# Value and output weights taken by halves of rows, inputs in quarters on two queues, and one more expert weight requested early

## The chip, the cores and the metric

The kernel runs on one core of a Trainium2 chip. The metric is the device time of one execution in microseconds; the median of three is 1227.86. TensorE (PE) does the matrix products, VectorE (DVE) and ScalarE (ACT) the elementwise work, GpSimd (POOL) a little of it, and SyncE (SP) issues nearly all loads.

## The reference, cut to what matters

All arrays are float32: 256 tokens, width 1024. The part around the change is the first mixer, and behind it a mixture of 32 experts and a second block.

```python
proj = h @ w_in[l] + b_in[l]          # 1024 x 5632
hg_q, hg_f, hg_i, hg_g, mb_q, mb_k, mb_v, gate_a, gate_b = jnp.split(proj, split_at, axis=-1)
y_a = hgrn2_mixer(hg_q, hg_f, hg_i, hg_g, ...) @ w_proj_a[l]
y_b = moba_mixer(mb_q, mb_k, mb_v, rel_bias) @ w_proj_b[l]
mixed = (jax.nn.sigmoid(gate_a) * y_a + jax.nn.sigmoid(gate_b) * y_b) @ w_out[l]
x = layer_norm(DN_ALPHA * h + mixed, ln1_g[l], ln1_b[l])
ffn = hier_moe(x, w_group[l], ...)    # 32 experts, two for each token
x = layer_norm(DN_ALPHA * x + ffn, ln2_g[l], ln2_b[l])
return second_block(x, ...)
```

## The kernel before, in words

All weights come as numbered units of 1 MB: unit i, 128 partitions x 2048 numbers. Units 0 to 25 are w_in and the two projections, 26 to 29 are w_out, and from E0 = 30 on come the experts' weights, 192 of them. For most units of the first stage a float32 product is made of three products in a rounded format (fp32r): ACT rounds the unit (`round_hi`, tile hi), DVE takes the rest (`rest_lo`, tile lo), and PE does hi*hi, hi*rest and rest*hi, 48 matmuls with 256 moving columns for one unit. Units 0 and 1 go through PE directly, out of tile xraw (x transposed) and raw. There are three buffers for hi and three for lo, six (raw0 to raw5) for the units themselves.

Most units are stationary on PE, with x moving. Those whose result has the tokens on partitions are moving instead: values i (4, 5), values mv (10, 11) and w_out (26 to 29). Each of these is a slice of 256 columns by all 1024 rows. `moving` does one such tile, `project_n` calls it for the values, `out_tile(j, i, k0, k1)` does slice j of w_out for half i of the tokens and rows from 128*k0 to 128*k1. Between rows 0 to 511 and 512 to 1023 of slice 0, PE does 18 small matmuls with the router's weights (WRG, called S12 below, L663 and L664).

DVE works in the order of the code: it copies S12 out of PSUM (L2046), then makes lo of units 27, 28 and 29 (L1850), then adds the residual for tokens 0 to 127 (L2118) once slices 0 to 3 of that half are done, norms, and goes on to the router.

SP issues loads strictly in order. A load into a buffer waits until its last user has left it: a raw buffer of the first stage is left when lo of its unit is made. The experts' units have a ring of 21 buffers: nine "spare" ones in areas of the first stage (semaphores early0 to early8), the six raw ones, and six "half" ones in the areas of hi and lo. Units E0 to E0+2 go to spare buffers once the attention is done; E0+3 to E0+6 go to raw0 to raw3, each behind lo of units 24 to 27; then E0+7 and E0+8 to spare ones. From E0+21 on a load waits for PE to have used the unit of 21 places before.

At the start SP issues half of x, half of unit 0, the other half, then unit 1; ACT issues the other half of x. PE keeps itself busy with four products of zeros (L533) until these are in.

Of the kernel before, what the change touches and what calls it, by code (L numbers as in the profile page):

```python
# [137 lines left out]
def weight_units(t):  # L138
# [17 lines left out]
    for j in range(4):  # L156
        units.append(("w_out", j, tcols(t["w_out"], (0, D), 256 * j, 256), 256, 8))
# [40 lines left out]
def memory(nc, t):  # L198
# [122 lines left out]
    K.RO = [sb(f"RO{n}", 1024, A0 + 40 * KB + 4 * KB * n) for n in range(4)]  # L321
    K.RZ = sb("RZ", 1024, A0 + 56 * KB)
# [126 lines left out]
def moving(pe, K, i, o, ks, xh, xl, start=True, stop=True):  # L449

    h, l, n = K.hi[i % HN], K.lo[i % HN], K.units[i][3]
    for c, k in enumerate(ks):
        pe.matmul(o, xh(k), K.view(h, n * c, [[1, 256]]), start=start and c == 0, stop=False)  # L453
        pe.matmul(o, xl(k), K.view(h, n * c, [[1, 256]]), start=False, stop=False)  # L454
        r = pe.matmul(o, xh(k), K.view(l, n * c, [[1, 256]]), start=False, stop=stop and c == len(ks) - 1)  # L455
    return r


def pe_mixers(pe, K, S):
# [72 lines left out]
    for n in range(4):  # L532
        pe.matmul(bank(7, 0, [1, 256]), view(K.QE, 0, [[1, 128]]), view(K.QE, 0, [[1, 256]]), start=True, stop=True)  # L533
# [100 lines left out]
    def out_tile(j, i, k0, k1):  # L634
        n = 26 + j
        if i == 0 and k0 == 0:
            lo_done(pe, K, S, n)
        b = 4 + 2 * i + j // 2
        h, l = K.hi[n % HN], K.lo[n % HN]
        if b == 7:  # L640
            pe.wait_ge(S.dve_step, STEP["s12"])
        for k in range(k0, k1):
            if j == 0 and k % 2 == 0:
                pe.wait_ge(S.mx_lo, k // 2 + 1)
            x, y = (view(m, 256 * k + 128 * i, [[1, 128]]) for m in (K.MXH, K.MXL))
            o = bank(b, 256 * (j % 2), [1, 256])
            pe.matmul(o, x, view(h, 256 * k, [[1, 256]]), start=k == 0, stop=False)
            pe.matmul(o, y, view(h, 256 * k, [[1, 256]]), start=False, stop=False)
            r = pe.matmul(o, x, view(l, 256 * k, [[1, 256]]), start=False, stop=k == 7)
        if k1 == 8 and i == 1:  # L650
# [1209 lines left out]
def dve_mixers(dve, K, S, own):  # L1860
# [3 lines left out]
    for n in range(2):  # L1864
        dve.wait_ge(S.early1 if n else S.early0, 16)
# [27 lines left out]
    def project(u):  # L1893
        dve_ahead(dve, K, S, u, K.E0)
        nm, j = K.units[u][:2]
        if nm in ("i", "mv"):
# [3 lines left out]
            dve.tensor_tensor(view(x, 256 * j, [[512, 2], [1, 256]]), bank(u % 3, 0, [256, 2], [1, 256]),  # L1900
                              view(K.BIA, (512 if nm == "mv" else 0) + 256 * j, [[0, 2], [1, 256]]), ALU.add).then_inc(S.pj_dve, 1)
# [209 lines left out]
def dve_router(dve, K, S, own):  # L2111
# [842 lines left out]
```

## Time and profile before

| | us |
|---|---|
| median of three executions | 1227.86 |
| lowest, highest | 1227.84, 1228.46 |
| the profiled execution | 1226.06 |
| its span on the core | 1224.8 |
| PE busy in it | 1093.8 |
| DVE busy in it | 581.4 |
| ACT busy in it | 476.8 |

Times in the trace count from the span's start. Three stages can be told apart: up to about 232 us the first mixer and the router, up to about 672 us the experts, and then the second block. PE's records overlap (one matmul of 256 columns lasts 0.28 us, but the next starts 0.12 us later), so pace is read from starts, not from durations.

### The profile page before, as it was taken

How to read it: one execution, taken by the hardware profiler on the slowest of the kernel's cores; microseconds unless marked ns; L12 is line 12 of the kernel's file. 1: busy time of each engine (PE TensorE's matmuls, PEld its weight loads, DVE VectorE, ACT ScalarE, POOL GpSimd, SP SyncE). 2: the span in 40 equal slices, each digit the busy share in tenths (PEclk: the TensorE clock that was granted, in tenths of full speed). 3: DMA queues.
4: the chain of work that ended last, by engine and by line, in shares of the span. 5: the costliest groups of instructions: out<-in, count | busy, mean ns of one | idle time of the engine just before them, and what ended most of it. 6: DMA issues, size and time to landing. Idle time of an engine off the chain costs nothing.

```text
span 1224.8 us, 22361 instructions
## 1 busy us (share of the span) xinstructions
PE 1093.8 (89%) x9746; PEld 907.8 (74%) x9746; DVE 581.4 (47%) x856; ACT 476.8 (39%) x650; POOL 87.7 (7%) x92
## 2 busy tenths in 40 slices
PE   8999999997767666666678999999999999999998
PEld 7999999764333333332324799999999999999998
DVE  4765676633222121212112766564554547666643
ACT  5644763221111111111123744433357775544432
POOL 1440000000000000000000400000110005000011
PEclk9999999999797878887977999999999999999999
DMA  9943567999999999999999766544534236565520
GB/s 336 324 144 111 189 226 298 421 419 421 420 421 420 420 422 420 420 421 419 412 422 409 234 207 200 179 155 169 193 103 156 87 105 201 177 207 175 177 97 35
DMA packets 144688, 329.82 MB, mean 269 GB/s; under 512 B 5507, under 2 KB 115388, under 8 KB 119886
## 3 DMA queue, kind: packets, MB, share of 16 engines
q1 hardware_dynamic: 142528, 321.99, 69.6%
q10 hardware_dynamic: 1470, 4.29, 1.0%
q0 software_dynamic: 592, 2.10, 0.5%
q8 instruction: 78, 1.28, 0.4%
q14 instruction: 20, 0.16, 0.0%
HBM read 327.30 MB, written 1.06 MB: 268 GB/s over the span
## 4 chain that ended last, share of the span: by engine, by line
PE 64%; DMA 31%; DVE 2%; ACT 1%; issue 1%; SPq 0%; DVEq 0%; ACTq 0%
PE PS L443 15%; PE PS L444 15%; PE PS L445 15%; DMA half<-in_w_down_dram 11%; DMA half<-in_w_gate_up_dram 7%; DMA raw<-in_w_down_dram 5%; DMA spare<-in_w_down_dram 4%; DMA raw<-in_w_gate_up_dram 4%; PE PS L785 3%; PE PS L453 1%; PE PS L454 1%; PE PS L455 1%; PE PS L771 1%; PE PS L526 1%; DVE lo L1850 1%; PE PS L1265 1%
## 5 line engine op out<-in xcount | busy, mean ns | idle before, releaser
L1850 DVE TENSOR_TENSOR lo<-raw,hi 128x2048 fp32r<-128x2048 f32 (+1 forms) x112 | 253.1, 2266 | 141.6 <-ACT hi L1357 112.6
L1357 ACT CAST hi<-raw 128x2048 fp32r<-128x2048 f32 (+1 forms) x110 | 203.7, 1857 | 102.4 <-PE PS L445 90.1
L443 PE MATMUL PS<-AH,hi 128*128 128x256 f32 (+1 forms) x816 | 234.8, 288 | 1.3 <-DVE AL L2339 1.0
L445 PE MATMUL PS<-AH,lo 128*128 128x256 f32 (+1 forms) x816 | 232.6, 285 | 0.0
L444 PE MATMUL PS<-AL,hi 128*128 128x256 f32 (+1 forms) x816 | 232.3, 285 | 0.0
L443 PEld LDWEIGHTS PS<-AH,hi 128*128 128x128 f32 x816 | 153.9, 189 | 2.7 <-issue 1.0
L445 PEld LDWEIGHTS PS<-AH,lo 128*128 128x128 f32 x816 | 154.0, 189 | 0.0
L444 PEld LDWEIGHTS PS<-AL,hi 128*128 128x128 f32 x816 | 153.5, 188 | 0.4
L2267 DVE TENSOR_TENSOR Y<-PS,Y 32x256 fp32r<-32x256 f32 x128 | 53.9, 421 | 131.8 <-ACT Y L1562 128.8
L2258 DVE TENSOR_TENSOR T<-T,PS 64x256 f32<-64x256 f32 x32 | 13.5, 423 | 192.8 <-ACT T L1554 192.7
L444 PE MATMUL PS<-FL,hi 128*128 128x272 f32 (+1 forms) x352 | 100.3, 285 | 0.0
L443 PE MATMUL PS<-FH,hi 128*128 128x272 f32 (+1 forms) x352 | 100.0, 284 | 0.0
L445 PE MATMUL PS<-FH,lo 128*128 128x272 f32 (+1 forms) x352 | 99.8, 284 | 0.0
L1562 ACT CAST Y<-PS 32x256 fp32r<-32x256 f32 x128 | 46.4, 363 | 132.0 <-PE PS L785 128.0
L1554 ACT ACTIVATE T<-PS 64x256 f32<-64x256 f32 x32 | 12.1, 377 | 205.6 <-PE PS L785 205.6
L785 PE MATMUL PS<-raw,XS 128*32 128x256 f32 x720 | 54.5, 437 | 22.7 <-DMA raw<-in_w_gate_up_dram 22.5
L785 PE MATMUL PS<-half,XS 128*32 128x256 f32 x640 | 53.8, 479 | 23.3 <-DMA half<-in_w_gate_up_dram 20.4
L443 PE MATMUL PS<-XH,hi 128*128 128x256 f32 x256 | 74.5, 291 | 0.0
L785 PE MATMUL PS<-spare,XS 128*32 128x256 f32 x688 | 50.0, 420 | 26.4 <-DMA spare<-in_w_gate_up_dram 26.4
L445 PE MATMUL PS<-XH,lo 128*128 128x256 f32 x256 | 72.4, 283 | 0.0
L444 PE MATMUL PS<-XL,hi 128*128 128x256 f32 x256 | 72.4, 283 | 0.0
L445 PEld LDWEIGHTS PS<-FH,lo 128*128 128x128 f32 x352 | 66.4, 189 | 0.0
(419 smaller groups left out, 1950.1 us busy)
## 6 DMA issues: line engine op xcount, KB each, us to landing
raw<-in_w_gate_up_dram SPq DMA_DIRECT2D x45, 1024.0 KB, 27.0
spare<-in_w_gate_up_dram SPq DMA_DIRECT2D x43, 1024.0 KB, 26.7
half<-in_w_gate_up_dram SPq DMA_DIRECT2D x40, 1024.0 KB, 27.0
half<-in_w_down_dram SPq DMA_DIRECT2D x23, 1024.0 KB, 26.4
raw<-in_ffn_w_gate_dram SPq DMA_DIRECT2D x22, 1024.0 KB, 5.6
raw<-in_ffn_w_up_dram SPq DMA_DIRECT2D x22, 1024.0 KB, 5.6
raw<-in_w_in_dram SPq DMA_DIRECT2D x21, 1024.0 KB, 10.8
raw<-in_w_down_dram SPq DMA_DIRECT2D x21, 1024.0 KB, 27.6
```

Of the source, the lines that this page charges most:

```text
L443: pe.matmul(o, w(h, c), xh(k), start=start and c == c0, stop=False)
L444: pe.matmul(o, w(h, c), xl(k), start=False, stop=False)
L445: r = pe.matmul(o, w(l, c), xh(k), start=False, stop=stop and c == c0 + len(ks) - 1)
L453: pe.matmul(o, xh(k), K.view(h, n * c, [[1, 256]]), start=start and c == 0, stop=False)
L454: pe.matmul(o, xl(k), K.view(h, n * c, [[1, 256]]), start=False, stop=False)
L455: r = pe.matmul(o, xh(k), K.view(l, n * c, [[1, 256]]), start=False, stop=stop and c == len(ks) - 1)
L785: r = pe.matmul(bank(b, 0, [1, 256], p0=32 * c, rows=32), x, view(w[0], w[1] + 256 * c, [[1, 256]]), start=first, stop=last)
L1357: act.copy(K.view(K.hi[i % HN], 0, [[1, n]]), K.view(K.rbuf[i], 0, [[1, n]])).then_inc(S.hi, 1)
L1562: act.copy(view(K.Y, 256 * c, [[1, 256]], 64 * (e % 2), KEEP), bank(down_bank(e), 0, [1, 256], p0=32 * c, rows=KEEP)).then_inc(S.y_hi, 1)
L1850: r = e.tensor_tensor(K.view(K.lo[i % HN], 0, [[1, n]]), K.view(K.rbuf[i], 0, [[1, n]]), K.view(K.hi[i % HN], 0, [[1, n]]).bitcast(F32), A ...
L2258: dve.tensor_tensor(K.T1[:, :], K.T1[:, :], bank(GB + e % 2, 0, [1, 256], p0=64, rows=64), ALU.mult).then_inc(S.hm, 1)
L2267: dve.tensor_tensor(l, bank(down_bank(e), 0, [1, 256], p0=32 * c, rows=KEEP), h.bitcast(F32), ALU.subtract).then_inc(S.y_lo, 1)
```

## The change

The units of values i and mv and of w_out become 512 rows by 512 columns instead of 1024 rows by 256 columns, so PE runs 24 matmuls of 512 moving columns for each instead of 48 of 256. A pair of values' units now fills two PSUM banks, one for each half of tokens, and DVE takes both out after the second unit. For w_out, units 26 and 27 are rows 0 to 511 (columns 0 to 511, and 512 to 1023), 28 and 29 are rows 512 to 1023. S12 stands behind both halves of tokens of unit 26. `w_in` is laid out in memory as 22 tiles that are contiguous for each partition (8 KB). The two halves of x and of unit 0 become four quarters each, x all on ACT's queue, unit 0 on SP's, and the zero products are three instead of four. E0+3 goes to a spare buffer with E0 to E0+2, and the raw buffers and all others shift by one place; areas of later tiles move so that this spare buffer is free. In the router, DVE adds the residual of tokens 128 to 255, columns 0 to 511, after the statistics of the first half of tokens.

```diff
+        w, c = (512, 4) if nm in ("i", "mv") else (256, 8)
         for j in range(2):
-            units.append((nm, j, tcols(win, (0, D), c0 + 256 * j, 256), 256, 8))
+            units.append((nm, j, win[c0 // 256 + j].rearrange("p (c n) -> p c n", c=c), w, c))
...
-        units.append(("w_out", j, tcols(t["w_out"], (0, D), 256 * j, 256), 256, 8))
+        units.append(("w_out", j, tcols(t["w_out"], (512 * (j // 2), 512 * (j // 2) + 512), 512 * (j % 2), 512), 512, 4))
...
-    ring = early[:3] + own[:4] + early[3:5] + own[4:] + early[5:]
+    ring = early[:4] + own[:4] + early[4:5] + own[4:] + early[5:]
...
-    for c, k in enumerate(ks):
-        pe.matmul(o, xh(k), K.view(h, n * c, [[1, 256]]), start=start and c == 0, stop=False)
+    for c, k in enumerate(ks, c0):
+        pe.matmul(o, xh(k), K.view(h, n * c, [[1, n]]), start=start and c == c0, stop=False)
...
-    for n in range(4):
+    for n in range(3):
         pe.matmul(bank(7, 0, [1, 256]), view(K.QE, 0, [[1, 128]]), view(K.QE, 0, [[1, 256]]), start=True, stop=True)
...
-    out_tile(0, 0, 0, 4)
-    out_tile(0, 1, 0, 4)
+    out_tile(0, 0)
+    out_tile(0, 1)
...
-    out_tile(0, 0, 4, 8)
-    out_tile(0, 1, 4, 8)
-    out_tile(1, 0, 0, 8)
-    out_tile(1, 1, 0, 8)
-    out_tile(2, 0, 0, 8)
-    out_tile(3, 0, 0, 8)
-    out_tile(2, 1, 0, 8)
+    out_tile(1, 0)
+    out_tile(1, 1)
+    out_tile(2, 0)
+    out_tile(3, 0)
+    out_tile(2, 1)
 
     pe.wait_ge(S.mx_mul, 8)
-    for n, (i, k0, k1) in enumerate(TURNS[:2]):
-        turn_rows(pe, K, S, n, i, k0, k1)
-    out_tile(3, 1, 0, 8)
+    turn_rows(pe, K, S, 0, *TURNS[0])
+    out_tile(3, 1, 0, 2)
+    turn_rows(pe, K, S, 1, *TURNS[1])
+    out_tile(3, 1, 2, 4)
...
-    act.dma_start(half(K.xraw, 1), t["xT"][:, 1024:2048]).then_inc(S.early1, 16)
+    for q, sx in enumerate((S.early0, S.early1, S.early2, S.early3)):
+        act.dma_start(view(K.xraw, 512 * q, [[1, 512]]), t["xT"][:, 512 * q:512 * q + 512]).then_inc(sx, 16)
...
-    dve.wait_ge(S.unit, 28)
-    residual(1, 0, 512)
     dve.wait_ge(S.x1_r, 1)
     for c in range(2):
         r = dve.bn_stats(st(0, 6 * c, 6), rows(0, 512 * c, 512))
     factor(0, own(r))
+    dve.wait_ge(S.unit, 29)
+    residual(1, 0, 512)
...
-    sp.dma_start(view(K.xraw, 0, [[1, 1024]]), t["xT"][:, :1024]).then_inc(S.early0, 16)
+    for q, sw in enumerate((S.early4, S.early5, S.early6, S.early7)):
+        sp.dma_start(view(K.raw[0], 512 * q, [[w, 2], [1, w]]), w0[:, 2 * q:2 * q + 2, :]).then_inc(sw, 16)
...
-    for i in range(7):
+    for i in range(8):
         sp_load(sp, K, S, K.E0 + i)
```

PE, before, from the first matmul of w_out to the first of unit 27. In the names, hi_57 and lo_60 hold unit 26, hi_55 and lo_58 unit 27.

```order
L647 MATMUL PS<-hi_57,MXH 128x256 [waits mx_lo,lo]
...
L647 MATMUL PS<-hi_57,MXH 128x256 [waits mx_lo]
...
L663 MATMUL PS<-WRG,cm 128x80 [waits rows,cm,mo_lo,pool_step]
L663 MATMUL PS<-WRG,cm 128x80 x7
L664 MATMUL PS<-rowp,cm 128x40
L647 MATMUL PS<-hi_57,MXH 128x256 [waits mx_lo]
...
L647 MATMUL PS<-hi_55,MXH 128x256 [waits lo]
```

PE, after, the same place (L455 is the first line of `moving`).

```order
L455 MATMUL PS<-hi_57,MXH 128x512 [waits mx_lo,lo]
...
L664 MATMUL PS<-WRG,cm 128x80 [waits rows,cm,mo_lo,pool_step]
L664 MATMUL PS<-WRG,cm 128x80 x7
L665 MATMUL PS<-rowp,cm 128x40
L455 MATMUL PS<-hi_55,MXH 128x512 [waits lo]
L456 MATMUL PS<-hi_55,MXL 128x512
...
L455 MATMUL PS<-hi_55,MXH 128x512 [waits dve_step]
```

Before, 24 matmuls of 256 columns stand ahead of S12 and 24 between it and unit 27. After, 24 matmuls of 512 columns stand ahead of it and none between it and unit 27.

DVE, after, around S12 (tile S_106; lo_58, lo_59 and lo_60 are units 27, 28 and 29).

```order
L2048 TENSOR_TENSOR MXL<-SGA,MXH 128x512 [waits mx_hi] x2
L2051 TENSOR_SCALAR S_106<-PS 128x40 [waits pe_step]
L2052 COPY S_106<-PS 128x40
L1852 TENSOR_TENSOR lo_58<-raw_52,hi_55 128x2048 [waits unit,hi,raw3]
L1852 TENSOR_TENSOR lo_59<-raw_53,hi_56 128x2048 [waits unit,hi,raw4]
```

This order on DVE is that of before: lo of unit 27 still follows the copies of S12.

SP, after, the first loads of the experts (raw_49 to raw_52 are raw0 to raw3).

```order
L2669 DMA spare_188<-in_w_gate_up_dram 128x2048
L2669 DMA spare_189<-in_w_gate_up_dram 128x2048
L2669 DMA raw_49<-in_w_gate_up_dram 128x2048 [waits lo]
L2669 DMA raw_50<-in_w_gate_up_dram 128x2048 [waits lo]
L2669 DMA raw_51<-in_w_gate_up_dram 128x2048 [waits lo]
L2669 DMA raw_52<-in_w_gate_up_dram 128x2048 [waits lo]
L2669 DMA spare_190<-in_w_down_dram 128x2048 [waits mx_lo]
```

Before, spare_189 stood behind raw_52, the load that waits for lo of unit 27; now it stands ahead of raw_49.

## Rows read from the trace of the kernel before

**Rows 1.** The page, parts 1 and 2: busy share; GB/s in 40 slices.

```profile
PE 1093.8 (89%) x9746; PEld 907.8 (74%) x9746; DVE 581.4 (47%) x856; ACT 476.8 (39%) x650; POOL 87.7 (7%) x92
...
GB/s 336 324 144 111 189 226 298 421 419 421 420 421 420 420 422 420 420 421 419 412 422 409 234 207 200 179 155 169 193 103 156 87 105 201 177 207 175 177 97 35
```

**Rows 2.** The chain that ended last: start, us, what.

```profile
14.57 6.91 PE PS L478 x32
...
264.04 24.24 DMA spare<-in_w_down_dram
```

**Rows 3.** Windows, all engines: us, PE, PEld, DVE, ACT, POOL busy, PEclk, DMA, GB/s.

```profile
192.00:196.00 4.00, 4.00 (x37) 4.00 (x35) 3.25 (x5) 1.29 (x4) 1.85 (x2) 1.00 0.18 70
196.00:200.00 4.00, 4.00 (x34) 3.87 (x33) 3.08 (x5) 1.88 (x2) 0.00 (x0) 1.00 0.01 2
...
204.00:208.00 4.00, 4.00 (x36) 4.00 (x35) 1.06 (x1) 0.00 (x0) 0.00 (x0) 1.00 1.03 430
```

**Rows 4.** Timeline of the start: start us, us, engine, line, operation, count.

```profile
2.64 3.78 PE L533 MATMUL PS<-QE 128*128 128x256 f32 x8 [2.64 <-POOL KE L2566]
...
7.43 7.14 PE L471 MATMUL PS<-xraw,raw 128*128 128x256 f32 x32 [1.01 <-DMA raw<-in_w_in_dram]
```

**Rows 5.** Windows at the start, same columns.

```profile
3.00:4.00 1.00, 1.00 (x3) 0.81 (x3) 0.00 (x0) 0.00 (x0) 0.00 (x0) 1.00 1.03 406
```

**Rows 6.** Timeline of PE: values (256 columns), second block (272), experts (512).

```profile
36.39 0.28 PE L454 MATMUL PS<-hi,XL 128*128 128x256 f32 x1
36.51 0.28 PE L455 MATMUL PS<-lo,XH 128*128 128x256 f32 x1
...
729.75 0.29 PE L443 MATMUL PS<-AH,hi 128*128 128x272 f32 x1
...
730.88 0.29 PE L443 MATMUL PS<-AH,hi 128*128 128x272 f32 x1
...
265.11 0.85 PE L833 MATMUL PS<-Y,SEL 128*128 128x512 f32 x3
265.34 0.63 PE L833 MATMUL PS<-Y,SEL 128*128 128x512 f32 x2
```

**Rows 7.** Timeline of PE around S12.

```profile
195.36 0.90 PE L663 MATMUL PS<-WRG,cm 128*128 128x80 f32 x7
...
197.54 0.39 PE L647 MATMUL PS<-hi,MXH 128*128 128x256 f32 x1
```

**Rows 8.** Timeline of DVE, from the last rest of the mix to the last residual.

```profile
195.34 1.46 DVE L2043 TENSOR_TENSOR MXL<-SGA,MXH 128x512 fp32r<-128x512 f32 x2
197.64 0.20 DVE L2046 TENSOR_SCALAR S<-PS 128x40 f32<-128x40 f32 x1 [0.84 <-PE PS L664]
197.76 0.19 DVE L2047 COPY S<-PS 128x40 f32<-128x40 f32 x1
197.87 4.49 DVE L1850 TENSOR_TENSOR lo<-raw,hi 128x2048 fp32r<-128x2048 f32 x2
...
212.24 1.82 DVE L2118 SCALAR_TENSOR_TENSOR X<-xtok,PS 128x1024 f32<-128x1024 f32 x2 [7.17 <-PE PS L649]
...
219.30 0.69 DVE L2118 SCALAR_TENSOR_TENSOR X<-xtok,PS 128x512 f32<-128x512 f32 x1 [0.33 <-PE PS L649]
```

**Rows 9.** Timeline of SP: issues of the experts' loads E0, E0+6, E0+20, E0+21.

```profile
173.20 0.34 SPq L2664 DMA_DIRECT2D spare<-in_w_gate_up_dram  x1
...
200.18 0.33 SPq L2664 DMA_DIRECT2D raw<-in_w_gate_up_dram  x1
...
228.25 0.33 SPq L2664 DMA_DIRECT2D spare<-in_w_down_dram  x1
...
236.07 0.33 SPq L2664 DMA_DIRECT2D spare<-in_w_down_dram  x1
```

**Rows 10.** DMA issues of 228 to 229 us: KB, us from issue to landing.

```profile
spare<-in_w_down_dram SPq DMA_DIRECT2D x1, 1024.0 KB, 12.8
```

**Rows 11.** Windows in the router, columns as in rows 3.

```profile
226.00:227.00 1.00, 0.30 (x2) 0.00 (x0) 0.87 (x8) 0.00 (x0) 0.00 (x0) 1.00 1.05 434
...
228.00:232.00 4.00, 3.90 (x16) 2.85 (x15) 3.54 (x19) 0.20 (x1) 0.00 (x0) 0.58 1.01 422
```

More of the change, by code:

```diff
@@ L320, in memory @@
     K.OVX = sb("OVX", OVR, A0 + 8 * KB)
[L321 to L322 removed]
+    K.RO = [sb(f"RO{n}", 1024, A0 + 56 * KB + 4 * KB * n) for n in range(4)]
+    K.RZ = sb("RZ", 1024, A0 + 72 * KB)
     K.SCR = sb("SCR", 1024, A0 + 72 * KB)
@@ L380, in memory @@
     own = [(K.raw[i], f"raw{i}") for i in range(RN)] + [(halves[i], f"half{i}") for i in range(6)]
-    ring = early[:3] + own[:4] + early[3:5] + own[4:] + early[5:]
+    ring = early[:4] + own[:4] + early[4:5] + own[4:] + early[5:]
     K.rbuf, K.filled, K.slot_before = {}, {}, {}
-    count = {f"early{i}": 1 for i in range(4)}
+    count = {f"early{i}": 1 for i in range(8)}
     last = {"raw0": 0}
@@ L464, in first @@
     def first():
+        quarters = ((S.early0, S.early4), (S.early1, S.early5), (S.early2, S.early6), (S.early3, S.early7))
         for k in range(8):
-            if k % 4 == 0:
-                for n in (S.early1, S.early3) if k else (S.early0, S.early2):
+            if k % 2 == 0:
+                for n in quarters[k // 2]:
                     pe.wait_ge(n, 16)
@@ L632, in pe_mixers, with out_tile @@
             r.then_inc(S.unit, 1)
-    def out_tile(j, i, k0, k1):
+    def out_tile(j, i, c0=0, c1=4):
         n = 26 + j
-        if i == 0 and k0 == 0:
+        if i == 0:
             lo_done(pe, K, S, n)
-        b = 4 + 2 * i + j // 2
-        h, l = K.hi[n % HN], K.lo[n % HN]
-        if b == 7:
+        b = 4 + 2 * i + j % 2
+        if j == 1 and i:
             pe.wait_ge(S.dve_step, STEP["s12"])
[L642 to L650, printed above, removed]
+        if i == 0 and j % 2 == 0:
+            pe.wait_ge(S.mx_lo, j + 2)
+        r = moving(pe, K, n, bank(b, 0, [1, 512]), range(4 * (j // 2) + c0, 4 * (j // 2) + c1), lambda k: view(K.MXH, 256 * k + 128 * i, [[1, 128]]),
+                   lambda k: view(K.MXL, 256 * k + 128 * i, [[1, 128]]), start=j < 2, stop=j >= 2 and c1 == 4, c0=c0)
+        if c1 == 4 and i == 1:
             r.then_inc(S.unit, 1)
-        elif j == 3:
+        elif j == 3 and i == 0:
             r.then_inc(S.pe_step, 1)
-    out_tile(0, 0, 0, 4)
-    out_tile(0, 1, 0, 4)
+    out_tile(0, 0)
+    out_tile(0, 1)
     pe.wait_ge(S.pool_step, STEP["wrg"])
@@ L1864, in dve_mixers @@
     for n in range(2):
-        dve.wait_ge(S.early1 if n else S.early0, 16)
+        for q in (S.early2, S.early3) if n else (S.early0, S.early1):
+            dve.wait_ge(q, 16)
         dve.wait_ge(S.xh, n + 1)
@@ L1899, in project @@
             dve.wait_ge(S.rows, 32)
-            dve.tensor_tensor(view(x, 256 * j, [[512, 2], [1, 256]]), bank(u % 3, 0, [256, 2], [1, 256]),
-                              view(K.BIA, (512 if nm == "mv" else 0) + 256 * j, [[0, 2], [1, 256]]), ALU.add).then_inc(S.pj_dve, 1)
+            for i in range(2):
+                dve.tensor_tensor(view(x, 512 * i, [[1, 512]]), bank((u - 1 + i) % 3, 0, [1, 512]),
+                                  view(K.BIA, 512 if nm == "mv" else 0, [[1, 512]]), ALU.add).then_inc(S.pj_dve, 1)
     def level_scale(n):
@@ L2679, in sp_first @@
     sp.wait_ge(S.mo_pv, 4)
-    for i in range(7):
+    for i in range(8):
         sp_load(sp, K, S, K.E0 + i)
     sp.wait_ge(S.mx_lo, 4)
-    for i in range(7, 11):
+    for i in range(8, 11):
         sp_load(sp, K, S, K.E0 + i)
@@ L2921, in layout @@
     x = g["x"]
+    w_in = g["w_in"][0].reshape(8, 128, 22, 256).transpose(2, 1, 0, 3)
+    tiles = [w_in[j].reshape(128, 2048) for j in range(22)]
+    for j in (4, 12):
+        for h in range(2):
+            tiles[j + h] = w_in[j:j + 2, :, 4 * h:4 * h + 4].transpose(1, 2, 0, 3).reshape(128, 2048)
     a = {
```

36 lines of the change are left out of this document (18 added, 18 removed).

## The prediction

> **What bounds the kernel now.** I read the page's busy shares and its slices first. PE is busy 89% of the span, but the slices of DMA traffic stand at 420 GB/s for a third of it and more [rows 1]: from about 215 us to 670 us the core does nothing but stream the experts' weights. The chain of waits says the same: up to the router it is PE, and from 264 us it goes from load to load [rows 2]. So there are two rules for what an edit is worth. Ahead of the stream, PE sets the time; inside it only bytes count, and a microsecond gained on PE is worth what it lets the loads run earlier. The second block is PE work again and starts when the last expert has landed, so a shift of the stream reaches the end undiminished.
>
> The reader should then look at where the stream starts. The experts' first load is issued at 173.20 and E0+6 at 200.18 [rows 9], and in between the queue runs dry: 70 GB/s from 192 to 196 us, 2 from 196 to 200 [rows 3]. 70 GB/s times 4 us are 0.28 MB, or 0.7 us at full rate, so data ends near 192.7 and is back at about 201. What reopens it is DVE: lo of unit 27 starts at 197.87 (two of them take 4.49) and E0+6 is issued at 200.18, 2.31 us after that start [rows 8, 9]. After 204 the queue is full [rows 3]. The place that decides is thus this hole of some 8 us, and when it closes.
>
> **The change part by part.** I keep two accounts: S, by how much everything up to the end of unit 25 comes earlier, and D, by how much the hole closes later against that shifted clock.
>
> Start. PE waits with zero products until 6.42 and begins at 7.43, released by unit 0's load [rows 4]. Eight passes take 3.78, 0.47 each, so two passes fewer end at about 5.5. It needed 1 MB of x and unit 0, and now needs half of that; at 406 GB/s [rows 5] 0.52 MB are 1.3 us, so data is there by 6.1 at the latest, and by 4.8 if the other halves that shared the way are counted too. I take 5.5, where the zero products end. Later quarters ask for 0.52 MB, 1.3 us, every eight passes, which take 1.8 us (7.14 for 32 [rows 4]), so they keep up. The zero products' pace (0.47) is half of that of the first real ones (0.22), so I read the lower level, 1.2 GHz, for them and 2.4 when L471 began, although the clock column shows 1.00 in both [rows 5]. Starting 1.9 earlier, part of the first passes will run at the lower level; up to 0.9 us of them, at half the pace, costs up to 0.5. Gain 1.9 less 0.5, 1.4; bounds 0.9 and 1.9. Unit 1 lands early enough in either case, since nothing in the chain stands between L471 and L478 (7.43 + 7.14 = 14.57 [rows 2, 4]).
>
> Values. Four units of 48 matmuls of 256 columns become 96 of 512. At 256 columns starts are 0.12 apart; at 272, 1.13 us hold nine, 0.126; so 16 columns cost 0.006, the pace follows the columns, and of the 0.12 some 0.013 are left that don't (256 at 2.4 GHz are 0.107). At 512 the experts' L833 shows 0.23 [rows 6]. A pair at 256 is 0.24, so each new matmul saves 0.010 and the four units 0.96. If only that rest goes, it is 96 x 0.013 = 1.25; if L833's 0.01 of rounding went the other way, nothing. I take 1.0.
> The Trainium skill, "TensorE: Matmul & The Clock Gate", section "Back-to-back issue gap", gives N/2.4 + 2.5 ns for a warm matmul. It would put 256 columns at 109 ns and 512 at 216, a saving of 2.5 ns a matmul and 0.24 us for the values. The trace differs at 256 (0.12 measured) and at 512 (0.23), so the rows decide; by the page the sum would be 0.7 us smaller for the values.
>
> Values' other edits cost nothing: DVE takes 1024 columns out after the second unit rather than 512 after each, the same work, and PE comes back to those banks only two units, over 11 us, later. S = 1.4 + 1.0 = 2.4.
>
> w_out and S12. In times of before (subtract 2.4 for those to come): 24 matmuls of 256 stood ahead of S12, 2.88 us, and it began at 195.36 [rows 7]. Now 24 of 512 stand there, 24 x 0.23 = 5.52, so S12 begins at 198.0 and PE is through with it 2.18 later (195.36 to 197.54 [rows 7]), at 200.2. DVE copies S12 0.10 after that and only then starts lo of unit 27, 0.33 after PE's end (197.54 to 197.87 [rows 7, 8]): 200.5, and 2.31 later, at 202.8, unit 27 is ready. Before, 24 matmuls lay between S12 and unit 27 and hid it almost exactly (197.54 + 2.88 = 200.42, against 200.18). Now nothing does: PE stands still from 200.2 to 202.8, 2.6 us. And behind that DVE instruction waits the load into raw3: the hole closes at 202.8 instead of 200.18. D = 2.6. DVE had been free from 196.8 (195.34 + 1.46), so it is the order of its queue that costs this, nothing else.
>
> The eighth early unit. E0+3 now joins the three behind 173.20 and needs no lo; E0+4 to E0+6 take the places of E0+3 to E0+5. At 421 GB/s one unit takes 1.05/421 = 2.5 us, and it runs in what was the hole: data ends at 195.2 instead of 192.7. When the hole closes, the stream has one unit more behind it. Worth 2.5. Bounds: 0 if the stream later has to wait anyway, 2.5 at most.
>
> Is there enough to load after the hole? E0+8 to E0+10 follow lo of units 28 and 29 (2.2 us each), E0+11 and E0+12 the end of unit 27 at 202.8 + 24 x 0.23 = 208.3, E0+13 the end of unit 28 at about 216.6. By then E0+7 to E0+12, six units or 15 us from 203.9, last until 218.9. It holds, with about 2 us to spare.
>
> The rest of w_out. From the start of unit 27 to the first residual there were 96 matmuls of 256, 11.52, from 200.42; now 48 of 512, 11.04, from 202.8: the residual on DVE goes from 212.24 to 214.1, 1.9 later. From there to the last residual DVE had 0.33 us of idle in 7.06 [rows 8], and its work is the same, so it ends at 220.9 or a little later, 1.6 to 1.8 later than 219.30; PE's own (2,1), turns and (3,1), 5.5 + 1.3 us, end at about the same time. So router and first expert come 1.7 late on the shifted clock. What waits for them is E0+21: it was issued at 236.07, while E0+20, issued at 228.25, landed 12.8 later at 241.05 [rows 9, 10]. That is 5.0 of lead, of which its own 2.5 of transport must be kept: 2.5 us of cover, and 1.7 fits under it.
>
> Sum: S 2.4, less D 2.6, plus 2.5 for the unit in the hole, 2.3; I take 2.2 for the little that DVE may add. The profiled execution goes from 1226.06 to 1223.9. The runs' median is 1.8 above that execution, so 1227.86 goes to 1225.7. A measurement of this kernel can tell about 0.2%, 2.5 us, from no change, and the forecast lies just inside that.
>
> **Rivals.**
> Clock: a stall of 2.6 us on PE may send its clock down. For it: after a microsecond with PE busy 0.30 [rows 11] the granted clock averaged 0.58 over 228 to 232, that is 3.4 of 4 us at 1.2 GHz. Against it: there PE had been lightly used before, here both sides are dense, and the 1.01 us gap before 7.43 did no harm. Price: 3.4 us at half pace lose 1.7, which makes the router 3.4 late; 2.5 is covered, 0.9 is not, so the gain is 1.3: 1226.6.
> No hold: unit 27 is ready in time after all, or the hole is paid for in another way (the clock at the start costs nothing, the pace at 512 follows the 0.013). Then D is near 0 and the gain 2.4 + 2.5 = 4.9: 1223.0. Against it: the order on DVE is fixed and its three durations are rows.
> Width gives nothing, 512 columns costing the 0.24 of two at 256: S is 1.4, the gain 1.3 or a little less: 1226.6. For it, that L833's 0.23 rests on single starts; it lies in the main case's own range. The Trainium skill's "TensorE: Matmul & The Clock Gate", section "Back-to-back issue gap", comes out near this.
> The other side, slower: the refill at E0+21. Each microsecond by which PE reaches the first expert later than 2.5 after the shifted clock empties the queue and is lost in full. It turns to a loss if that delay exceeds 2.5 + 2.2 = 4.7. PE at half pace through the rest of w_out would do it: the remaining 72 matmuls of 512 at 0.47 instead of 0.23 are 17 us, 12 to 14 net: 1240. If the clock is low for 7 us and not 3.4, the delay is 5.2, and the sum near zero. For it, the drop of rows 11; against it, that this drop ended while PE was dense.
>
> **How the numbers follow.** Main case 0.55, at 1225.7, with its own range of 1224.7 to 1226.9 from the bounds of start and width; about 0.2 of the 0.55 lies below 1225.4, which is faster by 0.2%. Clock 0.16, no change. No hold or a larger start gain 0.17, faster. Slower rival and what I do not see of that kind 0.12. So faster 0.37, same 0.51, slower 0.12. The range of 1222.6 to 1228.4 holds the main case, the clock case and most of the larger gains.
>
> **What would show it.** Right: L474 starts at 5.3 to 6.1; unit 6 starts 2 us earlier; PE idle of about 2.6 us between S12 and unit 27, released by DVE's lo; DMA near 0 GB/s for 8 us around 193 to 201; 421 GB/s from there on; the second block's first matmuls 2 to 2.5 us earlier. Wrong: unit 27 starting right behind S12, a granted clock under 1 between 200 and 206, a dip in GB/s near 216 or 238, or starts in L455 that are not 0.23 apart.

## The result, and the profile after

The changed kernel takes 1228.95 us (median of 18, 1228.08 to 1230.24), the kernel before 1226.46 beside it (18, 1225.89 to 1228.46): a ratio of 1.0015, interval 1.0009 to 1.0021. Forecast were 1225.7 and a gain of 2.2 us; by the ratio, which compares all the executions, it is 1.8 slower, and the two medians lie 2.5 apart. The profiled execution of the changed kernel has a span of 1227.5, that of before 1224.8. Every ratio below is against the kernel before, run beside the experiment; 0.001 is 1.2 us, and an interval is about 0.001 to either side.

The page's PE line and GB/s, which answer to [rows 1]:

```profile
PE 1099.1 (90%) x9552; PEld 900.1 (73%) x9552; DVE 580.8 (47%) x856; ACT 477.0 (39%) x650; POOL 90.5 (7%) x92
...
GB/s 358 286 152 116 187 228 295 397 420 420 420 421 421 420 420 420 421 420 420 412 420 411 244 194 199 192 149 164 202 94 162 90 104 198 181 206 171 179 97 35
```

PE is busy longer with fewer matmuls, and the eighth slice (214 to 245 us) has 397 GB/s where it had 421. So we look at two places: where PE got slower, and that slice.

The start, timeline of PE [rows 4], and the windows of that stretch (columns as in rows 3):

```profile
2.64 2.93 PE L538 MATMUL PS<-QE 128*128 128x256 f32 x6 [2.64 <-POOL KE L2571]
6.51 9.78 PE L474 MATMUL PS<-xraw,raw 128*128 128x256 f32 x32 [0.95 <-DMA xraw<-in_xT_dram]
```

```profile
2.00:3.00 1.00, 0.36 (x1) 0.36 (x2) 0.00 (x0) 0.00 (x0) 0.59 (x1) 1.00 0.87 127
3.00:4.00 1.00, 1.00 (x3) 0.81 (x3) 0.00 (x0) 0.00 (x0) 0.00 (x0) 1.00 0.66 127
4.00:5.00 1.00, 1.00 (x4) 0.67 (x2) 0.00 (x0) 0.00 (x0) 0.00 (x0) 1.00 0.82 223
5.00:6.00 1.00, 0.57 (x2) 0.00 (x0) 0.00 (x0) 0.00 (x0) 0.00 (x0) 1.00 1.04 324
```

Unit 0 starts 0.92 earlier than before, not 1.9, and takes 9.78 us, not 7.14, so it ends at 16.29 instead of 14.57: 1.7 late, where 1.4 early was forecast. The eight loads of 256 KB begin at 127 GB/s; the loads of before had 406 from 3 to 4 us [rows 5]. (Behind them the re-laid `w_in` is read faster: 417 GB/s from 9 to 35 us, for 360 before.)

The values, timeline of PE from their first matmul to the unit that follows, before (first fence) and after:

```profile
33.65 0.39 PE L453 MATMUL PS<-hi,XH 128*128 128x256 f32 x1
...
46.08 0.36 PE L443 MATMUL PS<-XH,hi 128*128 128x256 f32 x1
```

```profile
35.37 0.50 PE L455 MATMUL PS<-hi,XH 128*128 128x512 f32 x1
35.71 0.39 PE L456 MATMUL PS<-hi,XL 128*128 128x512 f32 x1
...
37.77 0.39 PE L456 MATMUL PS<-hi,XL 128*128 128x512 f32 x1
...
47.20 0.36 PE L445 MATMUL PS<-XH,hi 128*128 128x256 f32 x1
```

12.43 us before and 11.83 after: 0.60 for one pair of units, 1.2 for both, with 1.0 forecast. The pace is 2.06 / 9 = 0.229 [rows 6].

w_out, PE and DVE after, around S12 [rows 7, 8]:

```profile
200.32 0.41 PE L665 MATMUL PS<-rowp,cm 1*128 1x40 f32 x2
203.33 0.80 PE L455 MATMUL PS<-hi,MXH 128*128 128x512 f32 x1 [2.60 <-DVE lo L1852]
```

```profile
200.77 0.20 DVE L2051 TENSOR_SCALAR S<-PS 128x40 f32<-128x40 f32 x1 [3.42 <-PE PS L665]
200.89 0.19 DVE L2052 COPY S<-PS 128x40 f32<-128x40 f32 x1
201.00 6.69 DVE L1852 TENSOR_TENSOR lo<-raw,hi 128x2048 fp32r<-128x2048 f32 x3
...
215.97 1.22 DVE L2123 SCALAR_TENSOR_TENSOR X<-xtok,PS 128x1024 f32<-128x1024 f32 x1 [8.29 <-PE PS L457]
```

The hold is there as forecast: PE idle for 2.60. What follows it is in the windows of the changed kernel (columns as in rows 3):

```profile
192.00:196.00 4.00, 4.00 (x24) 3.47 (x24) 2.71 (x5) 1.29 (x2) 1.85 (x2) 1.00 0.89 369
196.00:200.00 4.00, 4.00 (x26) 3.57 (x25) 1.26 (x2) 3.69 (x3) 0.00 (x0) 1.00 0.03 10
200.00:204.00 4.00, 1.40 (x8) 1.11 (x8) 3.23 (x4) 1.92 (x2) 0.00 (x0) 0.87 0.00 0
204.00:208.00 4.00, 4.00 (x14) 3.20 (x13) 3.68 (x2) 0.00 (x0) 0.00 (x0) 0.70 0.88 326
...
220.00:224.00 4.00, 4.00 (x28) 3.52 (x27) 3.93 (x5) 1.17 (x2) 0.00 (x0) 1.00 0.90 346
224.00:228.00 4.00, 4.00 (x32) 3.78 (x31) 3.76 (x12) 2.17 (x4) 0.00 (x0) 1.00 0.95 334
```

The early unit fills 192 to 196 (369 GB/s for 70 [rows 3]). Behind the hold the granted clock is 0.87 and 0.70: about 2.9 us at half pace. And at 220 to 228 the queue runs short, (420-346) x 4 + (420-334) x 4 = 0.64 MB, 1.5 us of the stream.

### The profile page after: what moved, and what is told of

It is laid out like the page before. It is cut to its first block, busy times and chain, and to the rows that moved or that the text cites. A ratio compares the mean times of both kernels' runs of the same rounds, so it can differ in the third digit from the quotient of the medians.

```text
span 1227.5 us, 21978 instructions
## 1 busy us (share of the span) xinstructions
PE 1099.1 (90%) x9552; PEld 900.1 (73%) x9552; DVE 580.8 (47%) x856; ACT 477.0 (39%) x650; POOL 90.5 (7%) x92
## 4 chain that ended last, share of the span: by engine, by line
PE 65%; DMA 29%; DVE 3%; ACT 1%; issue 1%; SPq 0%; DVEq 0%; ACTq 0%
PE PS L445 15%; PE PS L446 15%; PE PS L447 15%; DMA half<-in_w_down_dram 11%; DMA half<-in_w_gate_up_dram 7%; DMA spare<-in_w_gate_up_dram 5%; PE PS L785 4%; DMA raw<-in_w_down_dram 4%; DMA raw<-in_w_gate_up_dram 2%; PE PS L455 2%; PE PS L457 2%; PE PS L456 2%; PE PS L531 1%; PE PS L771 1%; DVE lo L1852 1%; PE PS L474 1%
## 5 line engine op out<-in xcount | busy, mean ns | idle before, releaser
L785 PE MATMUL PS<-raw,XS 128*32 128x256 f32 x768 | 59.9, 446 | 24.4 <-DMA raw<-in_w_gate_up_dram 24.4
```

The source lines that it names most:

```text
L785: r = pe.matmul(bank(b, 0, [1, 256], p0=32 * c, rows=32), x, view(w[0], w[1] + 256 * c, [[1, 256]]), start=first, stop=last)
```

## The experiments

**Both losses, one at a time.** All four ran beside the same kernel before, whose 29 executions had a median of 1227.99.

```diff
-    for n in range(3):        # e1_warm4 and e4_warm4_lo27, on the changed kernel
+    for n in range(4):
-    for n in range(4):        # e2_before_warm3, on the kernel before
+    for n in range(3):
+    rest_lo(dve, K, S, 27)    # e3_lo27 and e4_warm4_lo27, DVE, ahead of the wait for S12
     dve.wait_ge(S.pe_step, STEP["s12_mm"])
...
-    for i in range(27, K.E0):
+    for i in range(28, K.E0):
```

> The changed kernel with four zero products at the start instead of three, nothing else. Theory A (the missing fourth product leaves the clock at 1.2 GHz when unit 0 begins): unit 0 still begins at about 6.5 us, takes 7.2 to 7.6 us instead of 9.78, and everything behind it comes 2.2 to 2.6 earlier; the time is 2.3 us under the changed kernel's. Rival B (the quarters' loads come in too slowly and PE waits between them): unit 0 still takes 9 us or more and the time stays within 0.5 us.

Measured: 1228.27, ratio 1.0007 (0.9998 to 1.0016).

> The kernel before with three zero products instead of four. Theory A: unit 0 begins at 7.43 as before but at half pace for 4 to 5 us, it takes 9.5 to 10 us instead of 7.14, and the time is 2.3 to 2.7 us over the kernel before. Rival B: unit 0 takes 7.2 us and the time does not move.

Measured: 1228.72, ratio 1.0006 (0.9997 to 1.0015).

> The changed kernel with DVE's lo of unit 27 ahead of its copies of S12 instead of behind them. Theory A (the order on DVE makes the stall of 2.6 us, the stall brings the clock down, and both hold the loads back): no idle of PE between S12 and unit 27, clock 1.00 throughout, E0+7 issued near 199.7 instead of 203.3, the end of w_out 3.7 us earlier, no dips in GB/s near 220 and 226; the time is 3 to 4.5 us under the changed kernel's. Rival B (the hole is not what delays the stream): the stall goes and the time moves by less than 1 us.

Measured: 1225.05, ratio 0.9977 (0.9968 to 0.9986).

> Both edits of the two runs before on the changed kernel. Theory A: the two add up, since one lies ahead of the hole and the other closes it: 5.5 to 7 us under the changed kernel's, 3 to 4.5 under the kernel before. Rival B: one hides the other, less than 4 under the changed kernel's.

Measured: 1224.28, ratio 0.9976 (0.9965 to 0.9987).

The order of DVE is the larger loss: from 1.0015 to 0.9977, 4.6 us, with one line moved. DVE in that kernel (e3):

```profile
197.16 2.28 DVE L1852 TENSOR_TENSOR lo<-raw,hi 128x2048 fp32r<-128x2048 f32 x1
200.66 0.20 DVE L2052 TENSOR_SCALAR S<-PS 128x40 f32<-128x40 f32 x1 [1.23 <-PE PS L665]
```

and PE goes on at 200.56, right behind S12. The zero products fit neither theory. The fourth one brings unit 0 down to 7.51 us in e1, as A had it, but the time by 1.0 and not 2.3; in e2 one product less costs 0.7 and not 2.3 to 2.7, though unit 0 takes 9.12 there. With the order mended, the fourth product gives nothing (e4 against e3), and e4 is 4.8 us under the changed kernel, between what A and B had. Only the mended order stands clear of the intervals. That asked for another look at the start.

**The start as it was, and single parts.**

```diff
     # f1_oldstart, f2_oldstart_lo27: the changed kernel with x and unit 0 in halves and 4 zero products
+    sp.dma_start(view(K.xraw, 0, [[1, 1024]]), t["xT"][:, :1024]).then_inc(S.early0, 16)
+    sp.dma_start(view(K.raw[0], 0, [[w, c // 2], [1, w]]), w0[:, :c // 2, :]).then_inc(S.early2, 16)
+    sp.dma_start(view(K.raw[0], 1024, [[w, c // 2], [1, w]]), w0[:, c // 2:, :]).then_inc(S.early3, 16)
     # f2 beside it: rest_lo(27) ahead of S12, as in e3
     # f3_before_val512: the kernel before, with the change's project_n and moving
+                units.append((nm, j, tcols(win, (512 * j, 512 * j + 512), c0, 512), 512, 4))
     # f4_oldstart_wout256: f1 with the w_out units and out_tile of the kernel before
```

> The changed kernel with the start of the kernel before: x and unit 0 each in two loads of 512 KB on the queues they had, four zero products. Everything else of the change stays, the re-laid w_in too. Theory A (eight loads of 256 KB fill slowly: 127, 127, 223 and 324 GB/s in the four us from 2 on, where the kernel before shows 164, 406, 410 and 332, so unit 2 comes to ACT 2.3 us late, and three zero products leave TensorE at half pace in unit 0): unit 1 starts at 14.6 instead of 16.3, ACT's split of unit 2 begins by 15.1 instead of 17.4, no wait of TensorE near 34, so the row tiles after unit 4 stand 2.5 to 3 us earlier than in the changed kernel. The hold of unit 27 (2.6 us of idle TensorE near 200) stays. Time 1.5 to 2.5 us under the changed kernel, so 0 to 1 us under the kernel before. Rival B (only the zero product counts, as with four of them and the small loads, which gave 1.0 us): 1.0 us under the changed kernel and no more.

Measured: 1229.24 (1226.13 to 1231.49), ratio 1.0012 (1.0002 to 1.0022).

> The same, and DVE splits unit 27's low part before it copies the router's first sums. Theory A: both losses are gone: hold removed was worth 4.6 us by ratio, the start 1.5 to 2.5 on top, so 4 to 5.5 us under the kernel before (ratio 0.9955 to 0.9967). Rival C (the DMA supply of the experts binds once the hold is gone, so that an earlier first stage is not kept): the same time as with the changed start and unit 27 ahead, 0.9976 of the kernel before, and four zero products beside it, which gave nothing over it.

Measured: 1226.25, ratio 0.9986 (0.9977 to 0.9995).

> The kernel before with one part of the change: the values' four units as halves of rows, 512 columns moving; their loads straight from w_in as it was. Theory A: 96 matmuls of 512 columns instead of 192 of 256, 1.1 to 1.2 us less TensorE until unit 25, kept to the experts since nothing there idles: 1.0 us under the kernel before, ratio 0.9991. Rival C (the first stage's time is not what sets when the experts' weights land): within 0.3 us of it.

Measured: 1226.6, ratio 0.9989 (0.9980 to 0.9998).

> The changed kernel with the start and the w_out tiles of the kernel before: what is left of the change is the values' width, the re-laid w_in and the eighth early unit. Theory A: no hold, so against the kernel before 1.2 us of the values and whatever the eighth early unit brings (0 to 2.5): 1.2 to 3 us under it, 0.9976 to 0.9990; against the same with w_out by 512 and unit 27 ahead it is 1 to 3 us more, since 96 matmuls of 512 against 192 of 256 give w_out 1.2 us too. Rival D (w_out's width brings nothing once the order is right): the two agree within 0.5 us.

Measured: 1226.61, ratio 0.9991 (0.9982 to 1.0000).

Theory A holds for f3. At f4 it is just missed (0.9976 to 0.9990), and f4 is 0.6 us above f2, not 1 to 3. At f1 and f2 it fails, where C's 0.9976 is missed as well. ACT's split of unit 2 did begin early, at 14.18, as it had said, but the time did not follow. The trace of f1 shows what went wrong in it:

```profile
2.64 3.78 PE L537 MATMUL PS<-QE 128*128 128x256 f32 x8 [2.64 <-POOL KE L2567]
7.79 9.19 PE L473 MATMUL PS<-xraw,raw 128*128 128x256 f32 x32 [1.37 <-DMA raw<-in_w_in_dram]
...
209.31 0.63 PE L455 MATMUL PS<-hi,MXH 128*128 128x512 f32 x1
209.74 0.47 PE L456 MATMUL PS<-hi,MXL 128*128 128x512 f32 x1
210.05 0.40 PE L457 MATMUL PS<-lo,MXH 128*128 128x512 f32 x1
```

With four zero products and the loads in halves, unit 0 takes 9.19 all the same, and behind the hold (from 204.03) starts stay 0.43 apart until 209.7. The kernel before shows it too: all its executions that stood beside the five sets, 134 of them, fall into two groups, 56 below 1227 with a median near 1226.2, and 78 above with one near 1228.2 (a few lie between, at 1227.2 to 1227.6). Unit 0 at 2.4 GHz from its start, or only from about 12 us on, is 2.0 us. So I formed theory E: after an idle gap of PE the granted clock is left to chance. (No execution of the upper group of the kernel before was traced; that its unit 0 is slow is read from e2, at 1228.88, whose E0 is issued at 175.22 for 173.20.)

**The chance taken away.**

```diff
-    for n in range(4):        # g1_before_warm5 (before); g2_after_warm5 (changed, from 3); g4_warm5_lo27 (e3, from 3)
+    for n in range(5):
+    for n in range(11):       # g3_after_fill, on the changed kernel, ahead of out_tile(1, 0)
+        pe.matmul(bank(5, 0, [1, 512]), view(K.MXH, 0, [[1, 128]]), view(K.MXH, 0, [[1, 512]]), start=True, stop=True)
```

> The kernel before with five zero products at the start instead of four: TensorE then works until 7.4 us and unit 0 follows without the 1.0 us of idle time. Theory E (the two groups of times of the kernel before, near 1226.2 and near 1228.2 us, are executions in which unit 0 runs at 2.4 GHz from its start and executions in which it runs at 1.2 GHz until about 12 us; the idle time ahead of unit 0 is what leaves it to chance): one group near 1226.2, unit 0 in 7.1 us, median 1.0 to 2.0 us under the kernel before where that has a slow half (ratio 0.9984 to 0.9993). Rival F (the groups come from something else, such as the DMA rate in the experts): two groups 2 us apart as before, the same median within 0.5 us.

Measured: 1226.32 (1226.04 to 1227.27), ratio 0.9990 (0.9981 to 0.9999), one group; the kernel before beside it was 10 times in the lower group and 21 times in the upper.

> The changed kernel with five zero products instead of three, nothing else. Theory E: unit 0 starts at 7.4, 0.9 later than with three, and runs at 2.4 GHz throughout: unit 1 at 14.6 to 14.9 instead of 16.3; what TensorE gains is partly lost again at 34 us, where unit 2's late landing (17.4 at ACT) holds it. 1.0 to 1.5 us under the changed kernel (ratio to the kernel before 1.0003 to 1.0007). Rival F: no change, 1.0015.

Measured: 1227.86, ratio 1.0006 (0.9997 to 1.0015).

> The changed kernel with eleven matmuls of 512 columns put into the hold of TensorE near 200 us, whose sums are thrown away (it writes a PSUM bank that the next tile starts anew); 11 x 0.227 = 2.5 of the 2.6 us. The wait for unit 27's low part stays, only the clock should not fall. Theory G (the hold costs its 2.6 us and 1.4 to 2.8 us more by the clock after it): the w_out matmuls after it go 0.227 apart at once, router and experts 1.4 us earlier or more, time 1.4 to 2.8 us under the changed kernel: ratio 0.9992 to 1.0004. Rival H (the clock's share is hidden, since SP's loads and DVE set what follows): within 0.3 us of the changed kernel, 1.0013 to 1.0017.

Measured: 1227.72, ratio 1.0001 (0.9992 to 1.0010).

> The changed kernel with five zero products and unit 27's low part ahead of the router's copies. Theory E and G together: no slow start and no hold. Against four zero products and the same order (0.9976 of the kernel before, of whose seven executions the spread was 1223.6 to 1225.5) it should be 0 to 1 us faster: 0.9968 to 0.9976, one group. Rival C (the supply of the experts' weights sets the end once the hold is gone): 0.9976, as with three and with four zero products.

Measured: 1224.63 (1224.08 to 1225.68), ratio 0.9979 (0.9970 to 0.9989).

G holds and H falls: filling the hold with thrown-away work is worth 1.7 us although it ends no earlier, and that is the clock's share. E holds at g1 and F falls there; g2 is inside E's range, with F's 1.0015 at the end of its interval, and g4's 0.9979 is just outside E's 0.9968 to 0.9976. PE in g3, and its window after the hold (the changed kernel had 0.70 there):

```profile
199.48 2.77 PE L667 MATMUL PS<-MXH 128*128 128x512 f32 x11
202.15 0.50 PE L455 MATMUL PS<-hi,MXH 128*128 128x512 f32 x1
202.49 0.40 PE L456 MATMUL PS<-hi,MXL 128*128 128x512 f32 x1
```

```profile
204.00:208.00 4.00, 4.00 (x20) 3.30 (x19) 2.50 (x2) 0.00 (x0) 0.00 (x0) 1.00 0.98 412
```

Unit 0 in all traces:

| idle before unit 0 | its length in us |
|---|---|
| 0.6 or less (e1, e4, g1, g2, g4, h1, h2, h3) | 7.1 to 7.8; g4's 7.8 hold a wait of 0.5 for x |
| 0.95 to 1.9 (before, g3, f4) | 7.14, 7.19, 7.14 |
| 0.95 to 1.9 (after, e3, e2, f1, f2, f3) | 9.78, 9.56, 9.12, 9.19, 8.76, 9.09 |

Long gaps go either way, short ones went well all eight times. The number of zero products is not what decides: with four of them unit 0 was fast in e1, e4, f4 and the kernel before, and slow in f1, f2 and f3. The hold behaves alike: of the five traces that have it, g2 kept its clock (2.59 of idle, then 0.227 a matmul), e1 and the changed kernel lost it for some 3 us, f1 for 5.7, and g3 filled it. The Trainium skill, "TensorE: Matmul & The Clock Gate", section "Part 1: The HAM clock gate (the "warmup" mystery)", says that what watches TensorE's activity runs on by itself and does not reset when a kernel starts; that fits a gap of one length that ends both ways here, though no trace shows the watcher itself.

What g4 doesn't show is a further gain: it is at 0.9979, with three and four zero products 0.9977 and 0.9976. That is rival C's number; whether for its reason, the last set shows.

**What was open: the early unit, the width, and the quarters.**

```diff
     # h2_before_warm5_early8: g1 with this of the change, its ring and its area moves
-    for i in range(7):
+    for i in range(8):
     # h3_before_warm5_val512: f3 with 5 zero products
     # h1_start_warm6_lo27: f2 with 6 zero products
```

> The changed kernel with the two-part start loads of the kernel before, six zero products and unit 27's low part ahead of the router's copies. With four zero products the same gave 0.9986 of the kernel before and its unit 0 ran at 1.2 GHz until past 12 us, after 1.4 us of idle time. Theory E (the idle time leaves the clock to chance, and each slow start costs up to 2 us): TensorE works until 8.3 us, unit 0 takes 7.1 us from there, ACT splits unit 2 at 14.2 and TensorE waits for nothing at 34: 0.9968 to 0.9976. Rival C (supply of the experts' weights sets the end): 0.9976 or above.

Measured: 1223.14 (5 executions, 1223.07 to 1224.68), ratio 0.9965 (0.9952 to 0.9978).

> The kernel before with five zero products, which takes chance out of its start (median 1226.3 us), and the eighth early unit alone of the change: its eighth expert unit is asked for with the first seven, and the areas move as in the change. Theory J (the 2.4 us of transfer that the unit fills the hole near 196 with are kept, since the experts' stage runs at the DMA's rate): 1224.0 to 1225.3 us. Rival K (the hole only moves, since SP then stands ahead of the ring's next free buffers with nothing to ask for): 1225.8 to 1226.8 us.

Measured: 1225.30, ratio 0.9984 (0.9976 to 0.9993).

> The kernel before with five zero products and the values by 512 columns alone: 1.17 us less TensorE by unit 25. Theory A: 1225.0 to 1225.4 us, 0.9 to 1.3 under the 1226.3 us with five zero products alone. Rival C: 1226.0 to 1226.6.

Measured: 1225.9, ratio 0.9983 (0.9974 to 0.9993).

h1 has the lowest time of all, 4.3 us under the kernel before by ratio, a little beyond what E expected, with C's 0.9976 still in its interval. Against g4 it has loads in halves instead of quarters, and one zero product more: 1.7 us by ratio, with intervals that overlap. In g4 ACT (first fence) gets unit 2 at 16.99, and PE waits for the fourth quarter of x and again near 34 us; in h1 (second fence) ACT has it at 14.17, and PE waits for nothing:

```profile
12.81 1.99 PE L474 MATMUL PS<-xraw,raw 128*128 128x256 f32 x8 [0.48 <-DMA xraw<-in_xT_dram]
...
16.99 1.90 ACT L1357 CAST hi<-raw 128x2048 fp32r<-128x2048 f32 x1 [1.17 <-DMA raw<-in_w_in_dram]
...
34.34 0.50 PE L455 MATMUL PS<-hi,XH 128*128 128x512 f32 x1 [0.39 <-DVE lo L1852]
```

```profile
7.92 7.51 PE L473 MATMUL PS<-xraw,raw 128*128 128x256 f32 x32
...
14.17 1.90 ACT L1356 CAST hi<-raw 128x2048 fp32r<-128x2048 f32 x1 [1.78 <-DMA raw<-in_w_in_dram]
```

So the quarters hold ACT and PE up early on. They don't explain the 1.7 us, though, for E0's load is issued no later with them (g4, then h1):

```profile
172.76 0.82 SPq L2670 DMA_DIRECT2D spare<-in_w_gate_up_dram  x2
```

```profile
172.90 1.70 SPq L2666 DMA_DIRECT2D spare<-in_w_gate_up_dram  x2
```

In the traces with wide values and a fast unit 0, E0 is issued at 172.1 to 173.3 with quarters (e1, e4, g2, g3, g4) and at 172.4 to 172.9 with halves (f4, h1, h3; h3 has the `w_in` of before). What makes h1's executions fast is not shown: there are five, and the traced one is their slowest.

**What one time mixes.** The traces can be cut where the stages meet. From PE's first matmul with PW (L863 before) to the end, all 17 take 547.9 or 548.0 us, so what differs lies ahead of it. The stretch from E0's issue to the landing of the last expert unit is free of the start:

| traces | E0's issue to the last landing, us |
|---|---|
| no early unit, no hold (before, e2, f3, g1, h3) | 498.2 to 498.6 |
| early unit, w_out as before (h2; f4) | 497.1; 498.3 |
| early unit and hold, the clock lost (the changed kernel, e1; f1) | 500.5, 500.4; 502.3 |
| early unit and hold, the clock kept or the hold filled (g2; g3) | 499.6; 499.0 |
| early unit, hold mended (e3, e4, f2, g4, h1) | 496.4 to 497.2 |

The last row answers rival C: e3's E0 is issued at 173.64 and g4's at 172.76, and their last units land at 670.64 and 669.62. What the first stage gains is kept.

Behind the last landing there is a second piece of chance. In 11 traces L863 follows it by 5.3 to 5.5 us, in six (e3, f2, g1, g2, g4, h3) by 6.1 to 6.5. The kernel before (first fence) and g1:

```profile
656.00:660.00 4.00, 3.40 (x32) 2.81 (x32) 0.14 (x1) 0.79 (x1) 0.00 (x0) 0.84 1.01 420
664.00:668.00 4.00, 4.00 (x39) 2.23 (x39) 0.71 (x2) 1.74 (x3) 0.00 (x0) 0.81 1.00 412
...
671.50 1.07 PE L785 MATMUL PS<-half,HTL 128*32 128x256 f32 x16 [0.58 <-DMA half<-in_w_down_dram]
```

```profile
656.00:660.00 4.00, 3.45 (x26) 1.78 (x22) 0.48 (x2) 1.16 (x1) 0.00 (x0) 0.50 1.01 422
664.00:668.00 4.00, 4.00 (x26) 2.05 (x18) 0.42 (x1) 1.86 (x3) 0.00 (x0) 0.60 1.01 418
...
671.80 1.93 PE L785 MATMUL PS<-half,HTL 128*32 128x256 f32 x32
```

In g1 the granted clock is low for longer, PE is late with the last experts, and the load that it waits for in the kernel before has already landed. This costs 0.8 to 1.1 us, and it comes with fast and slow starts alike (g1 and e3 have it). It fits the times between the two groups, and it makes single executions and medians of few hard to compare: g4 and h3 were traced in such an execution, e4 and h1 were not. So five zero products take away only the larger chance: of h3's executions five lie at 1224.7 to 1225.2 and five at 1225.85 to 1226.8.

The early unit alone brings 0.7 us by ratio and 1.0 by medians (0.9990 and 1226.32 to 0.9984 and 1225.30), and 1.1 in the table (h2), not 2.5; 1225.30 is the end of J's range with the least gain, and K's begins at 1225.8. In f4 it brings nothing in the table; there the clock fell in the router (0.59 from 228 to 232 us) and the queue ran short at 236 to 240 us (346 GB/s). h2's trace has the hole filled and a new dip where E0+13 should be on its way:

```profile
192.00:196.00 4.00, 4.00 (x36) 4.00 (x35) 3.21 (x5) 1.30 (x3) 1.85 (x2) 1.00 0.85 348
...
216.00:220.00 4.00, 4.00 (x37) 4.00 (x35) 3.64 (x4) 1.55 (x3) 0.00 (x0) 1.00 0.92 338
```

That dip is (420-338) x 4 = 0.33 MB, 0.8 us, in a kernel without any hold. e3 has 301 GB/s in the same window, 0.48 MB or 1.1 us. The width of the values alone is 0.9 us by ratio from g1 (0.9990 to 0.9983) and 1.3 as f3 (0.9989), which is theory A's figure; h3's median, 1225.9, lies between A's range and C's, and its E0 is issued at 172.43 for g1's 173.65. w_out's width has no run of its own: f2 and f4, which differ in it and in the order of DVE, are 0.6 us apart, less than their intervals. In their traces, E0+21 is issued 61.7 us after E0 in f2 and 62.9 in f4, so PE does gain 1.1 us there; how much of it reaches the end is open.

## Why the prediction was wrong, point by point

- **Base.** The forecast took the profiled execution of before as typical and carried its 1.8 us to the median along as a constant. It was an execution of the lower group, whose unit 0 ran fast; all three runs shown were of the upper one. The number was on the table and unexplained.
- **Start, 1.4 us gain: failed.** "It needed 1 MB of x and unit 0, and now needs half of that; at 406 GB/s": that rate belonged to loads of 512 KB. The quarters began at 127 GB/s, so data was there at 6.5, not 5.5. "Part of the first passes will run at the lower level ... costs up to 0.5": it was up to 2.6 (9.78 against 7.14). And later loads came late too, unit 2 at ACT at 17.4 instead of 15.1, which the sum had not counted; unit 6 came 1.1 us later, not 2 earlier. With three products unit 0 may be slow or fast (9.78 here, 7.19 in g3), and the forecast had no term for that chance. With a fast unit 0 the start is no gain either: E0's issue is at 172.1 to 173.3 with quarters and at 172.4 to 172.9 with halves. Whether the slow first loads come from their size or from their queues was not separated.
- **Values, 1.0: right.** 1.2 in the trace, 0.9 and 1.3 by the runs. The re-laid `w_in`, which the sum left out, shows no gain: 172.43 for E0 in h3 without it, 172.41 and 172.90 in f4 and h1 with it.
- **Hold, D = 2.6: right in place, cause and length**, and the order of DVE was its only cause. Mended, it gives 4.6 us, of which the fill shows 1.7 to be clock, so 2.9 for the hold itself. By the table of stretches it is 0.8 to 1.4 for the clock and some 2.5 for the hold.
- **Clock behind the hold, a rival at 0.16 and a price of 0.9: it happened.** Against it stood "the 1.01 us gap before 7.43 did no harm". One trace was read as a rule; that gap does harm in more than half of the executions. The price was low as well: 1.7 us by ratio, and PE late in w_out is not covered by the lead at E0+21 alone, since E0+13 is sooner in need.
- **Eighth early unit, 2.5: mis-sized.** Measured 0.7 to 1.1. "It holds, with about 2 us to spare" was wrong: it compared issue with the end of data, but a load needs some time of its own to land. In the changed kernel E0+7, issued at 203.31 into an empty queue, landed 4.8 us later, where its transport alone is 2.5; E0+13, issued at 218.68, landed at 224.74, 2.8 behind E0+12. This margin was gone without any hold.
- **Slower rival**: place (a late PE that empties the queue) right, but in the changed kernel at E0+13, not at E0+21, and it begins with no delay at all, not at 4.7 us. With the hold mended the queue runs short near E0+21 too (326 GB/s from 236 to 240 us in e4, 360 in e3).

By the experiments, then, and each to about 1 us: start 0 instead of -1.4, values -0.9, hold 2.9, its clock 1.7, early unit -0.7. That is 3.0, against the measured 1.8; the rest is within the errors of five ratios, or is the wider w_out, which has no run of its own.

The two traces add up better. In the changed kernel E0 is issued 0.55 us later (1.7 for the slow unit 0, less 1.2 for the values), the stretch to the last landing is 2.2 longer (hold and clock 3.2 to 4.0, less 1.1 for the early unit), and what follows is the same: 2.7 us, as the spans have it. So the steps that failed are the start (1.4 forecast, none found), the clock behind the hold (left out of the sum) and the early unit (2.5 forecast, about 1 found).

## What to carry to other kernels

When a wider tile is put ahead of a small step, ask which instruction of another engine used to hide behind the tiles between them; here one line of DVE's order was the difference between 1.8 us slower and some 3 faster. If a kernel's repeated times form two groups, settle what makes them before forecasting anything smaller than their distance, and compare traces stage by stage rather than by their ends. Keep TensorE busy up to the first real matmul, by enough dummy work to leave no gap. Before a load is split for the sake of an early start, read the rate at which such loads begin; and before counting on a load to be in time, add the time from its issue to its landing.

## What the runs showed of the hardware

- TensorE's clock after an idle gap: with gaps of 0.95 to 1.9 us three of nine traces went on at 2.4 GHz, six at 1.2 GHz until 11 to 12 us; with gaps of 0.6 or less all eight went fast; after 2.6 us one kept it, three did not, and it came back 2.9 to 5.7 us later. At the start the clock column stood at 1.00 in all of them, so only the pace shows it (passes 0.43 apart or 0.22).
- The granted clock near the experts' end differs between executions of like kernels: 0.84 from 656 to 660 us in the kernel before and 0.50 in g1. Six of 17 traces lose 0.8 to 1.1 us there.
- Eight loads of 256 KB on two queues: 127, 127, 223, 324 GB/s in the four us from 2 on; four loads of 512 KB, three of them on SP's queue: 164, 406, 410, 332. The Trainium skill, "DMA: Bandwidth & Descriptors", section "Measured (HBM→SBUF, 128 partitions, SWDGE, issued from GpSimd)", says to batch loads to a megabyte or more; the trace agrees in direction, on other queues, but size and queues were changed together.
- Matmuls of 512 columns of this kind start 0.229 us apart, of 256 0.12.
- A load of 1 MB that was issued into an empty queue landed 4.8 us later (E0+7 of the changed kernel).
